# Gates spread by 16-bit products in three parts, an input stage that starts from the unnormalised x, and a last norm in two halves

## The chip, the cores and the metric

The kernel runs on one core of a Trainium2 chip. The metric is the device time of one execution in microseconds (us). The engines of the core that matter here are TensorE (PE, matrix products into PSUM), VectorE (DVE), ScalarE (ACT), GpSimd (POOL) and SyncE (SP), which issues most of the transfers.

## What is computed

Two layers over 512 tokens of width 1024, each a mixer (a recurrence and a state-space part), a cross-attention to 256 memory rows, and a large key-addressed feed-forward layer, called peer; a norm closes the whole. Cut to what the change touches:

```python
def rmsnorm(x, g):
    y = xf * lax.rsqrt(jnp.mean(xf * xf, axis=-1, keepdims=True) + RMS_EPS)
    return (y * g.astype(jnp.float32)).astype(x.dtype)

h = rmsnorm(x, norm_mix[l]);  z = h @ w_in[l]          # input stage of the mixer
...
top, pos = lax.top_k(cand, PEER_TOPK)                   # peer: 8 heads x 16 experts of 128 x 128
eidx = jnp.take_along_axis(cidx, pos, axis=-1)
gate = jax.nn.softmax(top, axis=-1)
act = jax.nn.gelu(jnp.einsum('thkd,td->thk', ue, hc).astype(jnp.float32))
return jnp.einsum('thk,thkd->td', (gate * act).astype(ve.dtype), ve)
...
return rmsnorm(x, norm_final)
```

## The kernel before, in words

Activations lie transposed: 128 partitions are a slice of the features, and 512 tokens lie along the free axis. The order of each engine's work is written out by hand, and semaphores tie the engines together. Large fp32 products are made of three 32-bit-rounded ones: each operand is split in a high and a low part (`split_high` on ScalarE, line 195; `split_low` on VectorE, line 200) and `product` (lines 207 to 209) issues high x high, low x high, high x low.

**Input stage** (`front`). ScalarE squares x, TensorE sums the squares over the partitions with a matrix of ones (L358), VectorE makes the mean, ScalarE its root, VectorE the reciprocal (L503) and h = x * gain * rstd (L505), and both split h. Only then can the first of 18 weight tiles be multiplied (24 matmuls of 512 columns each). Two PSUM banks take the tiles in turn; ScalarE copies each result out (`take`, L416, or L411, which writes with a wide step, for the last four), and VectorE shifts, mixes and prepares the recurrence.

**Peer**. The layer is computed densely for 384 of the 512 tokens: 128 tiles of `peer_u` give the activations (phase up, 24 matmuls of 384 columns each), and 128 tiles of `peer_v` are added up with weights (phase down). The weights are gate times activation, so the 16 x 8 gates of a token have to be spread over a 128 x 128 table. That is done in the middle of phase up, for 24 groups of 16 tokens: `route` holds, for each of a token's 128 picks (the partition) the first key, the second key and the gate. VectorE makes a one-hot of the first key (`one`), a one-hot of the second key times the gate (`two`), each 128 x 2048 in fp32 (`make_onehots`, L2417 to L2419), and TensorE multiplies the two for each token (`spread_gates`, L2162): 16 matmuls a group, which in fp32 run as 32 passes. ScalarE moves the sums to `gates_out` (L2260), and SyncE stores them to HBM. Around this VectorE works in a fixed order: one-hots of the next group, the low part of one or two weight tiles (`lows`), one gathered expert row for the remaining 128 tokens (`rows`, L2352, fetched by GpSimd). TensorE works on one or two up tiles, then a spread, and so on; three groups come with four tiles.

**End**. `norm` works on all 512 tokens at once, then one transfer of 2 MB stores the output.

## Time and profile before

| | us |
|---|---|
| median of 2 runs (4155.95 and 4173.33) | 4164.64 |
| the profiled execution, its own time | 4179.48 |
| its span, first to last instruction | 4177.7 |
| TensorE busy | 3788.4 (91%) |
| VectorE busy | 3029.4 (73%) |
| ScalarE busy | 1375.9 (33%) |

Busy is the time in which an engine has an instruction in work; matmul records overlap each other, so that a busy TensorE need not be one at its peak. The granted clock of TensorE was 0.949 of full speed in the mean. The columns of each view are told with its first rows below.

### The profile page before, as it was taken

The page shows a single profiled execution, that of the slowest core. Times are in us where ns is not written, and L with a number is a line of the kernel's source. Part 1 is how long each engine was busy: PE and PEld are TensorE (multiplying, and loading weights), DVE is VectorE, ACT ScalarE, POOL GpSimd, SP SyncE. Part 2 cuts the span into 40 slices and gives each one's busy share as a digit, 9 for nine tenths or more (in the row PEclk, how much of TensorE's full clock was granted, in tenths as well). Part 3 has the DMA queues.
Part 4 walks back from the last instruction along what each step waited for, and adds up shares of the span by engine and source line. Part 5 has one row for each costly group of instructions (what it writes and reads, how often), then busy time and mean ns, then how long its engine had stood idle before and what let it go on. Part 6 is the DMA issues. An engine that isn't in the chain of part 4 may idle for free. (4 is left out here: it accounts for less than half of the span.)

```text
span 4177.7 us, 67901 instructions
## 1 busy us (share of the span) xinstructions
PE 3788.4 (91%) x27802; PEld 3460.6 (83%) x27802; DVE 3029.4 (73%) x5310; ACT 1375.9 (33%) x2109; POOL 869.4 (21%) x593
## 2 busy tenths in 40 slices
PE   6878889899998998999999888989999999999997
PEld 4547777699998998999986776669999898899996
DVE  6446455489888987877775646458888897877876
ACT  3442123333333432333334213333333343333332
POOL 3000000011102234444430000001111223544542
PEclk8989989999999999999999989999999999999998
DMA  4741212167776789999961022227777679999994
GB/s 151 262 144 35 99 54 99 61 206 206 208 209 208 270 319 355 338 337 343 349 246 61 22 99 71 91 72 220 211 209 212 213 264 335 359 342 340 338 340 183
DMA packets 319480, 885.61 MB, mean 212 GB/s; under 512 B 29473, under 2 KB 156577, under 8 KB 311745
## 3 DMA queue, kind: packets, MB, share of 16 engines
q1 hardware_dynamic: 245440, 612.80, 43.9%
q0 software_dynamic: 73728, 268.47, 18.0%
q8 instruction: 219, 3.59, 0.4%
q14 instruction: 93, 0.75, 0.1%
HBM read 751.13 MB, written 130.02 MB: 211 GB/s over the span
## 5 line engine op out<-in xcount | busy, mean ns | idle before, releaser
L207 PE MATMUL peer_ps<-peer_h_high,tile_high 128*128 128x384 f32 (+1 forms) x2304 | 797.3, 346 | 35.5 <-DVE peer_h_low L200 16.6
L207 PE MATMUL peer_ps<-gate_high,tile_high 128*128 128x384 f32 x2048 | 709.6, 347 | 96.9 <-DVE tile_low L200 96.8
L2120 POOL DMA_INDIRECT row<-in_peer_u_rows,row_at x256 | 380.9, 1488 | 1969.0 <-DVE row L2352 1202.1
L209 PE MATMUL peer_ps<-peer_h_high,tile_low 128*128 128x384 f32 (+1 forms) x2304 | 788.5, 342 | 0.0
L208 PE MATMUL peer_ps<-peer_h_low,tile_high 128*128 128x384 f32 (+1 forms) x2304 | 788.3, 342 | 0.0
L200 DVE TENSOR_TENSOR tile_low<-tile,tile_high 128x1024 fp32r<-128x1024 f32 x544 | 662.4, 1220 | 157.0 <-ACT tile_high L195 152.2
L208 PE MATMUL peer_ps<-gate_low,tile_high 128*128 128x384 f32 x2048 | 704.0, 344 | 0.0
L209 PE MATMUL peer_ps<-gate_high,tile_low 128*128 128x384 f32 x2048 | 702.9, 343 | 0.0
L195 ACT ACTIVATE tile_high<-tile 128x1024 fp32r<-128x1024 f32 x544 | 571.2, 1050 | 20.1 <-DMA tile<-in_peer_u 19.9
L2120 POOL DMA_INDIRECT row<-in_peer_v,row_at x256 | 454.6, 1776 | 480.0 <-DVE own_sum L2358 437.3
L207 PEld LDWEIGHTS peer_ps<-gate_high,tile_high 128*128 128x128 f32 x2048 | 398.1, 194 | 107.6 <-DVE tile_low L200 107.5
L207 PEld LDWEIGHTS peer_ps<-peer_h_high,tile_high 128*128 128x128 f32 x2304 | 435.5, 189 | 58.3 <-issue 32.6
L209 PEld LDWEIGHTS peer_ps<-peer_h_high,tile_low 128*128 128x128 f32 x2304 | 435.1, 189 | 10.7
L208 PEld LDWEIGHTS peer_ps<-peer_h_low,tile_high 128*128 128x128 f32 x2304 | 435.6, 189 | 9.6
L195 ACT ACTIVATE gate_high<-weighed 128x384 fp32r<-128x384 f32 x256 | 134.6, 526 | 804.5 <-DMA tile<-in_peer_v 480.2
L208 PEld LDWEIGHTS peer_ps<-gate_low,tile_high 128*128 128x128 f32 x2048 | 398.1, 194 | 0.0
L209 PEld LDWEIGHTS peer_ps<-gate_high,tile_low 128*128 128x128 f32 x2048 | 397.3, 194 | 0.0
L2239 ACT ACTIVATE up_act<-peer_ps 128x384 f32<-128x384 f32 x240 | 118.6, 494 | 811.4 <-DMA acts<-up_act 561.6
L2358 DVE SCALAR_TENSOR_TENSOR own_sum<-row,row_dots,own_sum 128x1024 f32<-128x1024 f32 x254 | 324.8, 1279 | 5.6
L2352 DVE SCALAR_TENSOR_TENSOR row<-row,h_own 128x1024 f32<-128x1024 f32 x256 | 307.7, 1217 | 3.6 <-DMA row<-in_peer_u_rows,row_at 3.6
L200 DVE TENSOR_TENSOR gate_low<-weighed,gate_high 128x384 fp32r<-128x384 f32 x256 | 141.4, 552 | 229.6 <-ACT tile_high L195 228.9
L2162 PE MATMUL peer_ps<-onehot_gates,onehot 128*128 128x128 f32 x1536 | 183.4, 277 | 10.4 <-ACT gates_out L2260 10.4
(453 smaller groups left out, 5476.2 us busy)
## 6 DMA issues: line engine op xcount, KB each, us to landing
tile<-in_peer_u SPq DMA_DIRECT2D x256, 512.0 KB, 4.1
tile<-in_peer_v SPq DMA_DIRECT2D x256, 512.0 KB, 7.1
gates<-gates_out SPq DMA_DIRECT2D x24, 2048.0 KB, 10.1
gates_in<-gates SPq DMA_DIRECT2D x32, 1536.0 KB, 15.9
acts<-up_act SPq DMA_DIRECT2D x240, 192.0 KB, 4.4
act_in<-acts SPq DMA_DIRECT2D x240, 192.0 KB, 8.8
in_w<-in_w_in SPq DMA_DIRECT2D x36, 512.0 KB, 3.6
tile<-in_peer_wq SPq DMA_DIRECT2D x32, 512.0 KB, 4.8
```

The source lines that it names most:

```text
L195: return act.activation(out, value, ACT.Copy)
L200: return dve.tensor_tensor(out, value, high.bitcast(F32), ALU.subtract)
L207: pe.matmul(out, wh, mh, start=first, stop=False)
L208: pe.matmul(out, wh, ml, start=False, stop=False)
L209: return pe.matmul(out, wl, mh, start=False, stop=last)
L2120: pool.indirect_dma_start(row[n % NROW][:, :], None, table, bass.IndirectOffsetOnAxis(ap=row_at[:, n % ROWS:n % ROWS + 1], axis=0)) \
L2162: last = pe.matmul(ps[2 + n % GBANKS][:, t * NKEY:(t + 1) * NKEY], one[g % 2][:, 4 * c + t, :], two[g % 2][:, 4 * c + t, :], start=True, s ...
L2239: act.activation(up[i % 2][:, :], ps[m % NPS][:, 0:TD], ACT.Gelu_apprx_tanh).then_inc(taken.sem, 1)
L2352: last = dve.scalar_tensor_tensor(out=x, in0=x, scalar=1.0, in1=h_own[:, :], op0=ALU.mult, op1=ALU.mult, accum_out=dots[:, j:j + 1])
L2358: last = dve.scalar_tensor_tensor(out=own_sum[:, :], in0=x, scalar=dots[:, j:j + 1], in1=own_sum[:, :], op0=ALU.mult, op1=ALU.add)
```

## The change

Three edits that do not depend on each other.

**Gates.** `route`, the one-hots and the ramp of keys become bf16, and the token index becomes the innermost one of the one-hots ([128 keys, 16 tokens] instead of [16 tokens, 128 keys]). So that nothing of a gate is lost it is split in three bf16 parts (`share_gates`), VectorE multiplies the second one-hot by each part (three products in place of one), and TensorE adds three bf16 matmuls per token in PSUM, in place of one fp32 matmul of two passes. It reads both operands with a step of 16 elements, 32 bytes.

**Input.** The tiles are multiplied by x * gain; rstd, which depends on the token alone, is multiplied in when a result is taken out of PSUM, now by VectorE. The first tile goes ahead of the sum of squares on TensorE.

**Last norm.** Mean, root, reciprocal and scaling go by halves of 256 tokens, and the output is stored in eight pieces as they are made.

```diff
-def norm(pg, src, gain, dst, n, early=None):
+def final_norm(pg, out):
...
+        @block.sync
+        def _(sp):
+            for h in range(2):
+                for k in range(KD):
+                    sp.wait_ge(scaled.sem, scaled.at(h * KD + k + 1))
+                    if k % 2:
+                        sp.dma_start(out[:, k - 1:k + 1, halves[h]], y[:, k - 1:k + 1, halves[h]]).then_inc(stored.sem, 16)
+            sp.wait_ge(stored.sem, stored.at(16 * KD))
...
-            act.wait_ge(meaned.sem, meaned.at(1))
-            act.activation(root[:, :], rstd[:, :], ACT.Sqrt).then_inc(rooted.sem, 1)
+                act.activation(sq[:, k, :], pg.xT[:, k, :], ACT.Square).then_inc(squared.sem, 1)
+            for h in range(2):
+                act.wait_ge(meaned.sem, meaned.at(h + 1))
+                act.activation(root[:, halves[h]], rstd[:, halves[h]], ACT.Sqrt).then_inc(rooted.sem, 1)
...
-            for k in range(KD):
-                pe.wait_ge(squared.sem, squared.at(k + 1))
-                last = pe.matmul(ps[:, :], pg.c["ones"][:, :], sq[:, k, :], start=(k == 0), stop=(k == KD - 1))
-            last.then_inc(summed.sem, 1)
+            for h in range(2):
+                for k in range(KD):
+                    pe.wait_ge(squared.sem, squared.at(k + 1))
+                    last = pe.matmul(ps[h][:, :], pg.c["ones"][:, :], sq[:, k, halves[h]], start=(k == 0), stop=(k == KD - 1))
+                last.then_inc(summed.sem, 1)
...
+
+            def mean(h):
+                dve.wait_ge(summed.sem, summed.at(h + 1))
+                dve.tensor_scalar(rstd[:, halves[h]], ps[h][:, :], 1.0 / D, RMS_EPS, ALU.mult, ALU.add).then_inc(meaned.sem, 1)
+
+            mean(0)
+            for h in range(2):
+                dve.wait_ge(rooted.sem, rooted.at(h + 1))
+                link(dve.reciprocal(rstd[:, halves[h]], root[:, halves[h]]))
+                if h == 0:
+                    mean(1)
+                for k in range(KD):
+                    dve.scalar_tensor_tensor(out=y[:, k, halves[h]], in0=pg.xT[:, k, halves[h]], scalar=gain[:, k:k + 1],
+                                             in1=rstd[:, halves[h]], op0=ALU.mult, op1=ALU.mult).then_inc(scaled.sem, 1)
...
+            tile(0)
             for k in range(KD):
                 pe.wait_ge(squared.sem, squared.at(k + 1))
                 last = pe.matmul(ps[7][:, :], pg.c["ones"][:, :], sq[:, k, :], start=(k == 0), stop=(k == KD - 1))
...
             for j in range(IN_TILES):
-                tile(j)
+                if j:
+                    tile(j)
...
-            def take(j):
-                act.wait_ge(in_summed.sem, in_summed.at(j + 1))
...
+            def scaled_high(k):
+                act.activation(rh[:, k, :], pg.xT[:, k, :], ACT.Copy, scale=gain[:, k:k + 1]).then_inc(h_high_made.sem, 1)
...
+            for k in range(4):
+                scaled_high(k)
+            high(0)
+            for k in range(4, KD):
+                scaled_high(k)
             for k in range(KD):
                 act.activation(sq[:, k, :], pg.xT[:, k, :], ACT.Square).then_inc(squared.sem, 1)
-            for j in range(2):
-                high(j)
+            high(1)
+            high(2)
             act.wait_ge(meaned.sem, meaned.at(1))
             act.activation(root, rstd, ACT.Sqrt).then_inc(rooted.sem, 1)
-            high(2)
-            for k in range(KD):
-                act.wait_ge(h_scaled.sem, h_scaled.at(k + 1))
-                split_high(act, rh[:, k, :], h[:, k, :]).then_inc(h_high_made.sem, 1)
             for j in range(IN_TILES):
-                take(j)
                 if j + IN_SPLIT < IN_TILES:
                     high(j + IN_SPLIT)
...
-                split_low(dve, rl[:, k, :], h[:, k, :], rh[:, k, :]).then_inc(h_low_made.sem, 1)
+                dve.scalar_tensor_tensor(out=rl[:, k, :], in0=pg.xT[:, k, :], scalar=gain[:, k:k + 1], in1=rh[:, k, :].bitcast(F32),
+                                         op0=ALU.mult, op1=ALU.subtract).then_inc(h_low_made.sem, 1)
...
+            def take(j):
+                i = IN_ORDER[j]
+                dve.wait_ge(in_summed.sem, in_summed.at(j + 1))
+                if i >= RW_TILES:
+                    tokens = lambda x: x.rearrange("p (n s) -> p n s", s=SC)
+                    dve.tensor_tensor(uT[:, i - RW_TILES, :].rearrange("p (s n) -> p n s", s=SC), tokens(ps[j % 2][:, :]), tokens(rstd),
+                                      ALU.mult).then_inc(in_taken.sem, 1)
+                    return
+                if j >= IN_ZB:
+                    dve.wait_ge(shifted.sem, shifted.at(j - IN_ZB + 1))
+                dve.tensor_tensor(zb[j % IN_ZB][:, 1:T + 1], ps[j % 2][:, :], rstd, ALU.mult).then_inc(in_taken.sem, 1)
...
+            for k in range(4):
+                h_left(k)
             weight_low(0)
+            for k in range(4, KD):
+                h_left(k)
+            weight_low(1)
             dve.wait_ge(summed.sem, summed.at(1))
             dve.tensor_scalar(rstd, ps[7][:, :], 1.0 / D, RMS_EPS, ALU.mult, ALU.add).then_inc(meaned.sem, 1)
-            weight_low(1)
+            weight_low(2)
...
             dve.wait_ge(rooted.sem, rooted.at(1))
             link(dve.reciprocal(rstd, root))
-            for k in range(KD):
-                dve.scalar_tensor_tensor(out=h[:, k, :], in0=pg.xT[:, k, :], scalar=gain[:, k:k + 1], in1=rstd,
-                                         op0=ALU.mult, op1=ALU.mult).then_inc(h_scaled.sem, 1)
-                if k >= 2:
-                    h_left(k - 2)
-            h_left(KD - 2)
...
             for j in range(IN_TILES):
+                take(j)
                 if j < RW_TILES:
                     shift(j)
...
+PLANES = 3
...
-        route = buf("route", [P, 3, TD])
+        route = buf("route", [P, 2 + PLANES, TD], BF16)
+        gate_row = buf("gate_row", [P, TD])
...
-            one = [buf(f"onehot{b}", [P, GROUP, NKEY], own=own) for b in range(2)]
-            two = [buf(f"onehot_gates{b}", [P, GROUP, NKEY], own=own) for b in range(2)]
+            one = [buf(f"onehot{b}", [P, NKEY, GROUP], BF16, own=own) for b in range(2)]
+            two = buf("onehot_second", [P, NKEY, GROUP], BF16, own=own)
+            shares = [buf(f"onehot_gates{b}", [P, PLANES, NKEY, GROUP], BF16, own=own) for b in range(2)]
+            key_ramp = buf("key_ramp", [P, NKEY, GROUP], BF16, own=own)
+            left = buf("gates_left", [P, TD], own=own)
...
-                        last = pe.matmul(ps[2 + n % GBANKS][:, t * NKEY:(t + 1) * NKEY], one[g % 2][:, 4 * c + t, :],
-                                         two[g % 2][:, 4 * c + t, :], start=True, stop=True)
+                        for j in range(PLANES):
+                            last = pe.matmul(ps[2 + n % GBANKS][:, t * NKEY:(t + 1) * NKEY], one[g % 2][:, :, 4 * c + t],
+                                             shares[g % 2][:, j, :, 4 * c + t], start=(j == 0), stop=(j == PLANES - 1))
                     last.then_inc(spread.sem, 1)
...
-                        act.activation(route[:, :, tb * P:(tb + 1) * P], bank[:, 0:3, :], ACT.Copy).then_inc(flip_taken.sem, 1)
+                        act.activation(route[:, 0:3, tb * P:(tb + 1) * P], bank[:, 0:3, :], ACT.Copy)
+                        act.activation(gate_row[:, tb * P:(tb + 1) * P], bank[:, 2, :], ACT.Copy).then_inc(flip_taken.sem, 1)
...
+            def share_gates():
+
+                link(dve.tensor_tensor(left[:, :], gate_row[:, :], route[:, 2, :], ALU.subtract))
+                link(dve.tensor_copy(route[:, 3, :], left[:, :]))
+                link(dve.tensor_tensor(left[:, :], left[:, :], route[:, 3, :], ALU.subtract))
+                link(dve.tensor_copy(route[:, 4, :], left[:, :]))
...
             def make_onehots(g):
                 t = slice(g * GROUP, (g + 1) * GROUP)
                 if g >= 2:
                     dve.wait_ge(spread.sem, spread.at((g - 1) * (GROUP // 4)))
-                per_key = lambda j: route[:, j, t].rearrange("p (t k) -> p t k", k=1).to_broadcast([P, GROUP, NKEY])
-                keys_at = pg.c["ramp"][:, :].rearrange("p (t k) -> p t k", t=1).to_broadcast([P, GROUP, NKEY])
-                dve.tensor_tensor(two[g % 2][:, :, :], keys_at, per_key(1), ALU.is_equal)
-                link(dve.tensor_tensor(one[g % 2][:, :, :], keys_at, per_key(0), ALU.is_equal))
-                last = dve.tensor_tensor(two[g % 2][:, :, :], two[g % 2][:, :, :], per_key(2), ALU.mult)
+                per_key = lambda j: route[:, j, t].rearrange("p (k t) -> p k t", k=1).to_broadcast([P, NKEY, GROUP])
+                if g:
+                    dve.wait_ge(onehots_made.sem, onehots_made.at(g))
+                dve.tensor_tensor(two[:, :, :], key_ramp[:, :, :], per_key(1), ALU.is_equal)
+                link(dve.tensor_tensor(one[g % 2][:, :, :], key_ramp[:, :, :], per_key(0), ALU.is_equal))
+                for j in range(PLANES):
+                    last = dve.tensor_tensor(shares[g % 2][:, j, :, :], two[:, :, :], per_key(2 + j), ALU.mult)
                 last.then_inc(onehots_made.sem, 1)
...
+            share_gates()
+            link(dve.tensor_copy(key_ramp[:, :, :], pg.c["ramp"][:, :].rearrange("p (k t) -> p k t", t=1)
+                                 .to_broadcast([P, NKEY, GROUP])))
             make_onehots(0)
```

How the instructions move. On VectorE in peer, one group of 16 tokens and what follows it (the numbers behind the names are those of buffers; `row` is a gathered expert row, `tile` a weight tile). Before:

```order
L2417 TENSOR_TENSOR onehot_gates_209<-ramp,route 128x2048 [waits spread]
L2418 TENSOR_TENSOR onehot_207<-ramp,route 128x2048
L2419 TENSOR_TENSOR onehot_gates_209<-onehot_gates_209,route 128x2048 [waits vec_step]
L200 TENSOR_TENSOR tile_low_168<-tile_162,tile_high_165 128x1024 [waits tile_high_made]
L2352 SCALAR_TENSOR_TENSOR row_184,row_dots<-row_184,h_own 128x1024 [waits row_loaded5]
L2417 TENSOR_TENSOR onehot_gates_210<-ramp,route 128x2048 [waits spread]
```

and in the changed kernel:

```order
L2453 TENSOR_TENSOR onehot_second<-key_ramp,route 128x2048 [waits onehots_made,spread]
L2454 TENSOR_TENSOR onehot_209<-key_ramp,route 128x2048
L2456 TENSOR_TENSOR onehot_gates_212<-onehot_second,route 128x2048 [waits vec_step]
L2456 TENSOR_TENSOR onehot_gates_212<-onehot_second,route 128x2048 x2
L210 TENSOR_TENSOR tile_low_169<-tile_163,tile_high_166 128x1024 [waits tile_high_made]
L2380 SCALAR_TENSOR_TENSOR row_186,row_dots<-row_186,h_own 128x1024 [waits row_loaded5]
L2453 TENSOR_TENSOR onehot_second<-key_ramp,route 128x2048 [waits onehots_made,spread]
```

Three instructions of a group have become five, the first of them waits also for the group before.

On TensorE, one spread with the last matmul of the tile ahead of it. Before:

```order
L209 MATMUL peer_ps_229<-peer_h_high,tile_low_168 128x384
L2162 MATMUL peer_ps_230<-onehot_gates_209,onehot_207 128x128 [waits onehots_made]
L2162 MATMUL peer_ps_230<-onehot_gates_209,onehot_207 128x128 x3
L2162 MATMUL peer_ps_231<-onehot_gates_209,onehot_207 128x128 x4
L2162 MATMUL peer_ps_232<-onehot_gates_209,onehot_207 128x128 x4
L2162 MATMUL peer_ps_233<-onehot_gates_209,onehot_207 128x128 x4
```

and in the changed kernel, where 16 matmuls (in fp32 of two passes each) are 48:

```order
L219 MATMUL peer_ps_234<-peer_h_high,tile_low_169 128x384
L2189 MATMUL peer_ps_235<-onehot_gates_212,onehot_209 128x128 [waits onehots_made]
L2189 MATMUL peer_ps_235<-onehot_gates_212,onehot_209 128x128 x11
L2189 MATMUL peer_ps_236<-onehot_gates_212,onehot_209 128x128 x12
L2189 MATMUL peer_ps_237<-onehot_gates_212,onehot_209 128x128 x12
L2189 MATMUL peer_ps_238<-onehot_gates_212,onehot_209 128x128 x12
```

On VectorE at the start of the input stage, before:

```order
L200 TENSOR_TENSOR in_w_low_57<-in_w_51,in_w_high_54 128x1024 [waits tile_high_made]
L500 TENSOR_SCALAR v<-front_ps_71 128x512 [waits norm_summed]
L200 TENSOR_TENSOR in_w_low_58<-in_w_52,in_w_high_55 128x1024 [waits tile_high_made]
L503 RECIPROCAL v<-v 128x512 [waits norm_rooted]
L505 SCALAR_TENSOR_TENSOR mixT<-xT,vec,v 128x512 [waits vec_step]
L505 SCALAR_TENSOR_TENSOR mixT<-xT,vec,v 128x512 x2
L200 TENSOR_TENSOR in_rl<-mixT,in_rh 128x512 [waits act_high_made]
L505 SCALAR_TENSOR_TENSOR mixT<-xT,vec,v 128x512
L200 TENSOR_TENSOR in_rl<-mixT,in_rh 128x512 [waits act_high_made]
```

and in the changed kernel:

```order
L492 SCALAR_TENSOR_TENSOR in_rl<-xT,vec,in_rh 128x512 [waits act_high_made] x4
L210 TENSOR_TENSOR in_w_low_57<-in_w_51,in_w_high_54 128x1024 [waits tile_high_made]
L492 SCALAR_TENSOR_TENSOR in_rl<-xT,vec,in_rh 128x512 [waits act_high_made] x4
L210 TENSOR_TENSOR in_w_low_58<-in_w_52,in_w_high_55 128x1024 [waits tile_high_made]
L521 TENSOR_SCALAR in_rstd<-front_ps_72 128x512 [waits norm_summed]
L210 TENSOR_TENSOR in_w_low_59<-in_w_53,in_w_high_56 128x1024 [waits tile_high_made]
L528 RECIPROCAL in_rstd<-v 128x512 [waits norm_rooted]
L505 TENSOR_TENSOR zb_60<-front_ps_65,in_rstd 128x512 [waits tile_summed,cleared,vec_step]
L510 TENSOR_TENSOR wag<-zb_60 128x512 [waits tile_taken]
L511 SCALAR_TENSOR_TENSOR wag<-wag,vec,zb_60 128x512 [waits vec_step]
L210 TENSOR_TENSOR in_w_low_57<-in_w_51,in_w_high_54 128x1024 [waits tile_high_made]
```

The splits no longer wait for the norm; the mean and the reciprocal come behind them, and each result is taken by VectorE (L505) ahead of its shift.

## Rows read from the trace of the kernel before

**Rows 1.** The profile page, engines: busy us, share, instructions

```profile
PE 3788.4 (91%) x27802; PEld 3460.6 (83%) x27802; DVE 3029.4 (73%) x5310; ACT 1375.9 (33%) x2109; POOL 869.4 (21%) x593
```

**Rows 2.** Stretches while gates are spread: busy us, clock, DMA share, GB/s

```profile
core 0: us, PE busy (x) PEld busy (x) DVE busy (x) ACT busy (x) POOL busy (x), PEclk, DMA share, GB/s
1400.00:1420.00 20.00, 20.00 (x140) 20.00 (x139) 19.93 (x14) 10.05 (x18) 7.47 (x3) 1.00 0.78 272
```

**Rows 3.** Timeline, VectorE, spreading: start us, us, instruction, [idle before]

```profile
1407.96 2.28 DVE L2417 TENSOR_TENSOR onehot_gates<-ramp,route 128x2048 f32<-128x2048 f32 x1
1410.16 2.28 DVE L2418 TENSOR_TENSOR onehot<-ramp,route 128x2048 f32<-128x2048 f32 x1
1412.48 2.29 DVE L2419 TENSOR_TENSOR onehot_gates<-onehot_gates,route 128x2048 f32<-128x2048 f32 x1
1414.69 1.22 DVE L200 TENSOR_TENSOR tile_low<-tile,tile_high 128x1024 fp32r<-128x1024 f32 x1
1415.83 1.22 DVE L2352 SCALAR_TENSOR_TENSOR row<-row,h_own 128x1024 f32<-128x1024 f32 x1
...
1436.13 2.29 DVE L2417 TENSOR_TENSOR onehot_gates<-ramp,route 128x2048 f32<-128x2048 f32 x1
```

**Rows 4.** Timeline, TensorE: a 384-column product, then two spreads

```profile
1341.60 0.33 PE L207 MATMUL peer_ps<-peer_h_high,tile_high 128*128 128x384 f32 x1
...
1342.12 0.33 PE L207 MATMUL peer_ps<-peer_h_high,tile_high 128*128 128x384 f32 x1
...
1508.06 3.73 PE L2162 MATMUL peer_ps<-onehot_gates,onehot 128*128 128x128 f32 x32
...
1515.80 3.73 PE L2162 MATMUL peer_ps<-onehot_gates,onehot 128*128 128x128 f32 x32
```

**Rows 5.** Groups of instructions, VectorE, 2048 elements: busy us, mean ns

```profile
L2418 DVE TENSOR_TENSOR onehot<-ramp,route 128x2048 f32<-128x2048 f32 x48 | 109.6, 2283 | 0.0
...
L1638 DVE COPY s_keep<-s_small 128x2048 f32<-128x2048 f32 x1 | 1.2, 1226 | 0.0
```

**Rows 6.** Groups, ScalarE and VectorE, 512 elements, with and without a wide step

```profile
L416 ACT ACTIVATE zb<-front_ps 128x512 f32<-128x512 f32 x28 | 16.7, 598 | 104.9 <-PE front_ps L209 104.9
...
L411 ACT ACTIVATE mixT<-front_ps 128x512 f32<-128x512 f32 x8 | 8.8, 1094 | 52.3 <-PE front_ps L209 52.3
...
L1180 DVE TENSOR_TENSOR rk<-mixT,s_turns 128x512 f32<-128x512 f32 x8 | 8.8, 1097 | 12.2 <-ACT s_turns L1087 12.2
```

**Rows 7.** Timeline, start of the input stage, layer 0

```profile
229.83 4.27 ACT L432 ACTIVATE rk<-xT 128x512 f32<-128x512 f32 x8 [17.03 <-PEq L1248]
...
257.26 0.60 ACT L416 ACTIVATE zb<-front_ps 128x512 f32<-128x512 f32 x1 [2.37 <-PE front_ps L209]
```

**Rows 8.** Timeline, start of cross-attention, layer 0

```profile
659.62 2.56 ACT L1820 ACTIVATE xa_h_high<-xT,vec 128x512 fp32r<-128x512 f32 x4 [11.89 <-PEq L892]
...
673.33 7.03 PE L1788 MATMUL xa_ps<-xa_q,ones 128*128 128x512 f32 x16
...
679.79 0.79 PE L207 MATMUL xa_ps<-xa_h_high,xa_w_high 128*128 128x512 f32 x1
...
682.13 3.35 DVE L1913 RECIPROCAL xa_rstd<-xa_root 128x512 f32<-128x512 f32 x1
```

**Rows 9.** Timeline, last norm and store; the group of 256-element reciprocals

```profile
4149.92 4.27 ACT L166 ACTIVATE norm_sq<-xT 128x512 f32<-128x512 f32 x8 [18.18 <-PEq L2010]
...
4164.77 5.39 DVE L185 SCALAR_TENSOR_TENSOR yT<-xT,vec,norm_rstd 128x512 f32<-128x512 f32 x8
...
4171.03 0.34 SPq L2560 DMA_DIRECT2D out<-yT  x1
...
L1546 DVE RECIPROCAL mem_rstd<-mem_root 128x256 f32<-128x256 f32 x1 | 1.8, 1753 | 0.1
```

**Rows 10.** Timeline, VectorE, end of the input stage, layer 1

```profile
2338.77 2.28 DVE L564 TENSOR_TENSOR rk<-rk,cum 128x2048 f32<-128x2048 f32 x1
...
2353.01 2.48 DVE L580 TENSOR_TENSOR e<-front_ps,v 128x512 f32<-128x512 f32 x4
```

More of the change, by code:

```diff
@@ L361, in _ @@
             for j in range(IN_TILES):
-                tile(j)
+                if j:
+                    tile(j)
                 if j in LORA_AFTER:
                     if j == 5 and layer:
+                        pe.wait_ge(v1_scaled.sem, v1_scaled.at(1))
                         for k in range(KD):
-                            last = pe.matmul(ps[7][0:32, :], v1[:, k, :], h[:, k, :], start=(k == 0), stop=(k == KD - 1))
+                            last = pe.matmul(ps[7][0:32, :], v1[:, k, :], pg.xT[:, k, :], start=(k == 0), stop=(k == KD - 1))
                         last.then_inc(v1_summed.sem, 1)
@@ L526, in _ @@
                     link(last)
+                if j == 6 and layer:
+                    dve.wait_ge(v1_summed.sem, v1_summed.at(1))
+                    dve.tensor_tensor(vl[:, :], ps[7][0:32, :], rstd[0:32], ALU.mult).then_inc(v1_taken.sem, 1)
                 if j == 6:
@@ L581, in _ @@
                     link(last)
[L582 removed]
+    for s, n in ((squared, KD), (summed, 1), (meaned, 1), (rooted, 1), (v1_scaled, 1 if layer else 0), (h_high_made, KD), (h_low_made, KD),
                  (high_made, IN_TILES), (low_made, IN_TILES), (in_summed, IN_TILES), (in_taken, IN_TILES), (shifted, RW_TILES),
@@ L2552, in build @@
             peer(pg, layer)
[L2553 to L2561 removed]
+        final_norm(pg, out)
 def kernel(**inputs):
```

61 lines of the change are left out of this document (14 added, 47 removed).

## The prediction, made before the changed kernel ran

> **What bounds the kernel now.** I read the engines' shares first. TensorE is busy for 91% of the span and VectorE for 73% [rows 1], but these are means over stages, so I went to the three places that the change touches. While gates are spread, both are full: in a typical 20 us TensorE has 20.00 and VectorE 19.93 us of work in hand, at full clock, with DMA at 0.78 [rows 2]. Which of them sets the pace is read from their timelines. VectorE starts one-hots at 1407.96 and, three groups later, at 1436.13 [rows 3]: 28.17 us for three groups with four weight tiles, with no idle time noted. On TensorE two high x high products, three matmuls apart, start 0.52 us apart, so a 384-column matmul takes 0.173 us and a tile of 24 takes 4.15. From spread to spread with one tile between them it is 7.74 us [rows 4]; that leaves 3.59 for the 32 passes of a spread, 0.112 each. Three groups cost TensorE 4 x 4.15 + 3 x 3.59 = 27.4 us. So VectorE bounds this stage by 0.8 us in 28: the reader should see that a saving on VectorE alone is worth almost nothing, and that the price of a spread on TensorE decides. The stage is 24 groups in each of two layers, 16 times three groups, 450 us.
>
> At the start of the input stage TensorE waits for the norm: 27.4 us from the first square to the first tile taken [rows 7]. The end is a chain of one engine after the other [rows 9].
>
> **Gates, VectorE.** A group has three operations of 2.28 us that start 2.20 or, behind a wait for the one before, 2.32 apart; with the last, 6.73 us [rows 3]. They become five, of 16-bit elements. No row shows VectorE on such operands. The upper bound is the fp32 operation, 2.28 us for 2048 elements; the lower one is the fp32 copy, 1.23 us, two elements a step [rows 5]. I take the lower: the copy moves 8 bytes per element, in and out, and a product with three 16-bit operands moves 6. Then the five start 1.14 or 1.26 apart, 5.8 us, and a group gives back 0.9: three groups are 25.4 us. The Trainium skill (VectorE: DVE Perf Modes, The perf-mode tier table) has 1224 ns for a bf16 `tensor_tensor` of this size; no run here shows it yet.
>
> **Gates, TensorE.** 32 passes become 48 (the order shows 12 matmuls per bank for 4). What does a bf16 pass of 128 columns cost? The lower bound is by columns: 0.173 us for 384 is 0.058 for 128 if all scales; with some 0.01 that does not scale, 0.065. The nearest row by shape is the fp32 pass itself, 0.112. The upper bound comes from the wide step: ScalarE takes 1094 ns to write 512 elements with a step of 256 bytes and 598 without one, and VectorE 1097 ns to read 512 of them, nearly what 1024 plain ones take [rows 3, 6]. That is 1.0 ns more per element, or 1.8 to 2.1 in all; 128 columns are 0.19 us a pass if 1.0 ns is added to 0.065, and 0.24 at 1.85 ns in all. Both operands of the new matmuls have a step of 32 bytes. I take 0.065, since TensorE reads a 4-byte column in 0.42 ns where a bf16 column has 2 bytes, and both ends stay for the range. Three groups are then 4 x 4.15 + 144 x 0.065 = 26.0 us, above VectorE's 25.4, so TensorE would set the pace: 28.17 - 26.0 = 2.2 us, 16 times, **-35**. Not all of it comes: the split of the gates (four short operations), the ramp's copy (1.2 to 2.3 us) and ScalarE's three extra copies stand ahead of the first one-hots; less what the first group is quicker, that is about 3.5 us a layer, **+7**. Gates: -28. What follows, phase down, is unchanged and starts earlier by as much. ScalarE's work, 10 us in 20, and the stores cover nothing that becomes late.
>
> The Trainium skill (TensorE: Matmul & The Clock Gate, Back-to-back issue gap) gives about 81 ns for a matmul of 128 columns with its weight load. By that three groups are 16.6 + 11.7 = 28.3 us, and the gates would bring nothing. No pair of this kind is in the trace.
>
> **Input stage.** Cross-attention in this trace already works in the new order: scaled high parts first, tile 0, then the sum of squares. There tile 1 starts 20.2 us after ScalarE's first instruction (659.62 to 679.79), and the reciprocal ends at 25.9, before tile 1 is through [rows 8]. In the input stage tile 1 starts at 27.4 [rows 7]. I take the difference, 7.2 us a layer, **-14**. Against it: 18 takes move from ScalarE to VectorE, 0.7 us each and about 1.1 for the four with a wide step [rows 6]. Mostly TensorE's tiles (24 x 0.227 = 5.4 us) cover them. Where VectorE is the late one, in the middle of the stage, some 0.8 us a layer is added. At the end of layer 1 it works from 2338.77 to 2355.5 without a stop [rows 10], and the take of tile 15 now stands behind 9 us of it, while tile 17 waits for that bank: about 3 us. **+4.5** in all. The extra product on v1 is short and hidden by the wait for the root.
>
> **Last norm.** Now 20.2 us from the first square to the last scaled tile, then 0.9 to the issue and 6.7 to the end of the span [rows 9]. With halves: squares 4.3, root of half 0 by 6, reciprocal 1.75 [rows 9], scaling 3.2, a mean 0.4, then 1.75 + 3.2 for half 1: 16.3 us, and a last piece of 256 KB in place of 2 MB, perhaps 3.5 with its issue. 27.8 becomes 19.8, **-8**.
>
> **Sum** against the profiled execution: 4179.5 - 28 - 9.5 - 8 = 4134. That execution is 14.8 us above the median of the runs shown; on the median's footing it is 4164.6 - 45.5 = **4119**.
>
> **Rivals.**
> - *The gates bring nothing* (a pass at about 0.080): -10 to -18 us in all, about 4150. Against it, the column rate of rows 4; for it, that a weight load is no cheaper than it was.
> - *A bf16 pass costs as much as an fp32 one*, 0.112: 16.6 + 16.2 = 32.8 us for three groups, +74 us, with the rest 4221. For it: the weights of 128 columns are loaded in each pass, and the wide step may take back what 2-byte columns give.
> - *Slower*: the wide step costs TensorE per element what it costs the others. 0.19 to 0.24 a pass make 44 to 51 us of three groups, +250 to +370, so 4400 to 4515. It sets in, for the whole kernel, above 0.124 a pass, where the gates alone cost 100 us. For it, two engines agree on the price [rows 6]; against it, one of these is a write, both are fp32, and TensorE is another reader. The Trainium skill (SBUF — State Buffer, Specifications) says that full bandwidth needs at least two hits in each line of 16 bytes; a step of 32 bytes has one. Whether TensorE feels that, no row here shows.
> - *VectorE gains nothing from 16 bits*: 2 x 2.2 us more per group, 48 times, +211, with the rest 4360.
>
> **Chances.** The forecast's case 0.46, no gain from the gates 0.10, pass as before 0.24, wide step 0.13, VectorE at the old rate 0.07. The first three, 0.80, lie between 4085 (VectorE-bound, 44 us from the gates, the others a little better) and 4250, which is my range; the forecast's case by itself has 4085 to 4140. Two per cent, about what a measurement of this kernel can tell from no change, is 83 us: faster than 4081 has 0.08, a corner of the first case; slower than 4248 has 0.22, the last two cases and an edge of the third; within it 0.70.
>
> **What would show it.** The spread in the changed trace: 48 passes in about 3.1 us; 5.4 would be the second rival, 9 or more the third. VectorE's 2048-element operations at 1.22 us, or at 2.28. The distance of one-hot starts over three groups, 26.0. Tile 1 of the input stage 20 us after its start. At the end, 20 us from the first square. I am wrong if a pass is above 0.08, if TensorE's clock drops in the stage because it now waits, or if takes on VectorE hold tiles up elsewhere in the input stage.

## The result: 8.9% slower, and the profile after

The changed kernel takes 4534.98 us in the median of two runs (4531.09 to 4538.86), the kernel before 4164.64: a ratio of 1.089, with a 95% interval of 1.078 to 1.100. I had forecast 4119 with a range of 4085 to 4250. The profiled execution after is the one of 4538.86 us, against 4179.5 before: +359.4. It is the rival of the wide step that happened, a little dearer than I had priced it.

The page of the changed kernel: engines, the granted clock and DMA share in 40 slices, then the groups of the spread and of VectorE's first 16-bit operation of a group (busy us, mean ns, idle before and its releaser).

```profile
PE 4187.9 (92%) x28586; PEld 3661.5 (81%) x28586; DVE 3013.9 (66%) x5448; ACT 1376.2 (30%) x2079; POOL 791.8 (17%) x593
...
PEclk8899999999977779999999989999997777999999
...
L2189 PE MATMUL peer_ps<-onehot_gates,onehot 128*128 128x128 bf16 x2304 | 562.8, 423 | 3.9 <-DVE onehot_gates L2456 3.9
...
L2453 DVE TENSOR_TENSOR onehot_second<-key_ramp,route 128x2048 bf16<-128x2048 bf16 x48 | 58.8, 1225 | 414.8 <-PE peer_ps L2189 414.6
```

TensorE gained 400 us of busy time where [rows 1] has 3788.4, and VectorE fell from 73% to 66%. VectorE's operation takes 1225 ns where the fp32 one took 2283 [rows 5], as forecast. But ahead of the one-hots of a group it now waits for TensorE, 414.6 us in all. In the kernel before, the same wait came to 3.4:

```profile
L2417 DVE TENSOR_TENSOR onehot_gates<-ramp,route 128x2048 f32<-128x2048 f32 x48 | 109.7, 2286 | 3.5 <-PE peer_ps L2162 3.4
```

The clock has two troughs of four slices, and these are the two stages in which gates are spread.

TensorE's timeline in one of them (start us, us, instruction); a spread, five of the 24 products behind it and the next spread:

```profile
1411.64 11.71 PE L2189 MATMUL peer_ps<-onehot_gates,onehot 128*128 128x128 bf16 x48
1422.98 0.69 PE L217 MATMUL peer_ps<-peer_h_high,tile_high 128*128 128x384 f32 x1
1423.47 0.52 PE L218 MATMUL peer_ps<-peer_h_low,tile_high 128*128 128x384 f32 x1
1423.79 0.52 PE L219 MATMUL peer_ps<-peer_h_high,tile_low 128*128 128x384 f32 x1
...
1425.70 0.34 PE L219 MATMUL peer_ps<-peer_h_high,tile_low 128*128 128x384 f32 x1
1425.87 0.33 PE L217 MATMUL peer_ps<-peer_h_high,tile_high 128*128 128x384 f32 x1
...
1428.50 11.73 PE L2189 MATMUL peer_ps<-onehot_gates,onehot 128*128 128x128 bf16 x48
```

From the start of a spread to the next product is 11.34 us for 48 passes, **0.236 us each**; the spreads in [rows 4] were 3.73 us long. The products behind it start 0.32 us apart at first and 0.173 later. The clock explains that second, smaller loss. Stretches through the same spread (busy us of each engine, granted clock, DMA share, GB/s):

```profile
1413.00:1415.00 2.00, 2.00 (x10) 1.21 (x9) 1.85 (x3) 0.51 (x2) 0.00 (x0) 1.00 0.23 27
1415.00:1417.00 2.00, 2.00 (x10) 1.24 (x9) 0.00 (x0) 0.37 (x1) 0.94 (x1) 0.61 0.74 274
1417.00:1419.00 2.00, 2.00 (x10) 1.28 (x9) 0.00 (x0) 0.60 (x1) 0.00 (x0) 0.50 0.94 293
...
1423.00:1425.00 2.00, 2.00 (x8) 2.00 (x7) 1.61 (x2) 0.60 (x1) 0.00 (x0) 0.50 0.00 0
```

The clock is full (2.4 GHz) at the start of the spread and falls to half (1.2 GHz) some 4 us into it. Ten passes lie in or across each stretch of 2 us at either level (8.5 of them start in it, at 0.236 us each), so the pass doesn't wait for the array; it waits for something that the clock doesn't touch. What the low level costs comes afterwards: the tile behind a spread takes 5.5 us (1422.98 to 1428.50) in place of 4.15.

VectorE over one group (start us, us, instruction, [idle before and releaser]) has its work for a group done and waits for a buffer of the spread; the first line is the start of the group ahead, the last one that of the third group after it:

```profile
1406.68 1.23 DVE L2453 TENSOR_TENSOR onehot_second<-key_ramp,route 128x2048 bf16<-128x2048 bf16 x1 [11.86 <-PE peer_ps L2189]
...
1423.39 1.22 DVE L2453 TENSOR_TENSOR onehot_second<-key_ramp,route 128x2048 bf16<-128x2048 bf16 x1 [8.54 <-PE peer_ps L2189]
1424.53 1.22 DVE L2454 TENSOR_TENSOR onehot<-key_ramp,route 128x2048 bf16<-128x2048 bf16 x1
1425.78 3.50 DVE L2456 TENSOR_TENSOR onehot_gates<-onehot_second,route 128x2048 bf16<-128x2048 bf16 x3
...
1461.39 1.22 DVE L2453 TENSOR_TENSOR onehot_second<-key_ramp,route 128x2048 bf16<-128x2048 bf16 x1 [11.82 <-PE peer_ps L2189]
```

One-hots start at 1406.68 and, three groups later, at 1461.39: 54.7 us where [rows 3] gives 28.17.

**The balance**, read as the first and last start of the matmuls of each stage in both profiled executions. First to last spread: before 1304.8 to 1527.0 and 3269.8 to 3494.8 (222.2 and 225.0 us), after 1283.0 to 1712.9 and 3434.4 to 3863.3 (429.9 and 428.9): +411.6. Input stage, first ScalarE instruction to last product: -7.1 and -2.6. Last gate product to the end: -5.9. The scan stage, between the last product of the input and the first of the tail, which the change doesn't touch: 205.1 and 207.7 before, 193.0 and 193.1 after, -26.7. The small rest, -9.9, is spread over the other stages. 411.6 - 9.7 - 5.9 - 26.7 - 9.9 = +359.4. Two things were to be explained: the price of the pass, and 27 us that nobody had asked for.

### The profile page after: what moved, and what is told of

The parts are those of the page before. It is cut to its first block and busy times, and to the rows that moved or that the text cites. A ratio compares the mean times of both kernels' runs of the same rounds, so it can differ in the third digit from the quotient of the medians.

```text
span 4537.1 us, 69625 instructions
## 1 busy us (share of the span) xinstructions
PE 4187.9 (92%) x28586; PEld 3661.5 (81%) x28586; DVE 3013.9 (66%) x5448; ACT 1376.2 (30%) x2079; POOL 791.8 (17%) x593
## 5 line engine op out<-in xcount | busy, mean ns | idle before, releaser
L217 PE MATMUL peer_ps<-peer_h_high,tile_high 128*128 128x384 f32 (+1 forms) x2304 | 826.4, 359 | 24.8 <-DVE peer_h_low L210 16.4
L218 PE MATMUL peer_ps<-peer_h_low,tile_high 128*128 128x384 f32 (+1 forms) x2304 | 812.0, 352 | 0.0
L219 PE MATMUL peer_ps<-peer_h_high,tile_low 128*128 128x384 f32 (+1 forms) x2304 | 808.5, 351 | 0.0
L2146 POOL DMA_INDIRECT row<-in_peer_u_rows,row_at x256 | 310.4, 1213 | 2420.3 <-DVE row L2380 1668.3
L2189 PE MATMUL peer_ps<-onehot_gates,onehot 128*128 128x128 bf16 x2304 | 562.8, 423 | 3.9 <-DVE onehot_gates L2456 3.9
L2189 PEld LDWEIGHTS peer_ps<-onehot_gates,onehot 128*128 128x128 bf16 x2304 | 338.4, 149 | 212.3 <-issue 7.2
L217 PEld LDWEIGHTS peer_ps<-peer_h_high,tile_high 128*128 128x128 f32 x2304 | 456.7, 198 | 49.0 <-issue 25.7
L218 PEld LDWEIGHTS peer_ps<-peer_h_low,tile_high 128*128 128x128 f32 x2304 | 454.7, 197 | 9.6
L219 PEld LDWEIGHTS peer_ps<-peer_h_high,tile_low 128*128 128x128 f32 x2304 | 453.8, 197 | 10.7
L2453 DVE TENSOR_TENSOR onehot_second<-key_ramp,route 128x2048 bf16<-128x2048 bf16 x48 | 58.8, 1225 | 414.8 <-PE peer_ps L2189 414.6
```

Source lines behind the costliest of these rows:

```text
L217: pe.matmul(out, wh, mh, start=first, stop=False)
L218: pe.matmul(out, wh, ml, start=False, stop=False)
L219: return pe.matmul(out, wl, mh, start=False, stop=last)
L2146: pool.indirect_dma_start(row[n % NROW][:, :], None, table, bass.IndirectOffsetOnAxis(ap=row_at[:, n % ROWS:n % ROWS + 1], axis=0)) \
L2189: last = pe.matmul(ps[2 + n % GBANKS][:, t * NKEY:(t + 1) * NKEY], one[g % 2][:, :, 4 * c + t], shares[g % 2][:, j, :, 4 * c + t], start=( ...
L2453: dve.tensor_tensor(two[:, :, :], key_ramp[:, :, :], per_key(1), ALU.is_equal)
```

## Experiments

Theory: the pass costs 0.236 us because the elements of its operands lie 32 bytes apart. Rivals: 48 short 16-bit passes cost that by their number, weight loads or accumulation; or the low clock is the cause and not a consequence; or part of the loss sits in the input stage or the last norm.

### e1: gates as before, the other two parts as changed

```diff
-            one = [buf(f"onehot{b}", [P, NKEY, GROUP], BF16, own=own) for b in range(2)]
+            one = [buf(f"onehot{b}", [P, GROUP, NKEY], own=own) for b in range(2)]
...
-                        for j in range(PLANES):
-                            last = pe.matmul(..., one[g % 2][:, :, 4 * c + t], shares[g % 2][:, j, :, 4 * c + t], ...)
+                        last = pe.matmul(..., one[g % 2][:, 4 * c + t, :], two[g % 2][:, 4 * c + t, :], ...)
```

> The changed kernel with the gates of the kernel before (one-hots in fp32, one product a token, each token's 128 elements side by side), its input stage and its last norm as changed. Theory (the whole loss lies in the gates): the two stages 222 and 225 us from first to last spread as before, the rest as after, so 4539 - 412 = about 4127 us profiled, 0.985 to 0.993 of the kernel before. If the scan stage of the changed kernel was shorter only by the clock it happened to get (27 us over both layers), that may be missing: 4154. Rival (the input stage or the last norm costs part of it): above 4180.

Measured: 4137.55 us, ratio 0.9948 (0.9924 to 0.9973); profiled 4127.4. Spreads over 222.2 and 221.8 us. The whole loss is in the gates, and the other two parts together are a small gain, some 20 us. The profiled time is the one expected; the ratio lies just above the 0.985 to 0.993 that I had expected.

### e2 to e4: which operand's step is paid for

```diff
+flat = lambda x, n: x.rearrange("p k t -> p (k t)")[:, n * NKEY:(n + 1) * NKEY]
...
-                            last = pe.matmul(..., one[g % 2][:, :, 4 * c + t],
-                                             shares[g % 2][:, j, :, 4 * c + t], ...)
+                            last = pe.matmul(..., flat(one[g % 2][:, :, :], 4 * c + t),
+                                             flat(shares[g % 2][:, j, :, :], 4 * c + t), ...)
```

e2 has both edits, e3 only that of `one` (the weights), e4 only that of `shares` (the moving operand, the one that streams through the array). VectorE still writes the old layout, so the gates come out as other numbers and only the times of these three count.

> The changed kernel, all instructions the same, but TensorE reads both operands of the 48 passes of a group from 128 elements that lie side by side, so the gates are other numbers. Theory (the step of 32 bytes between elements is what a pass costs): pass 0.06 to 0.09 us, spread of a group 3 to 4 us in place of 11.4, three groups 26 to 28 us in place of 53.8, VectorE's wait for spreads gone, the clock of the tile behind a spread full; time 4539 - 16 x 27 = about 4105 to 4140 us. Rival (48 short passes in 16 bits cost this whatever the step, by their number, their weight loads or PSUM accumulation): 0.237 us a pass, 4535 us. Rival (the low clock is the cause): pass as at full clock from the start of a spread, which was 0.2 us too, so no change.

> As e2, but only the one-hots of the first keys, which are loaded as weights, are read side by side; the moving operand keeps its step of 32 bytes. If each operand pays for its own step and the reads follow one another (0.237 = 2 x 0.118): 0.17 to 0.18 us a pass, 8.4 us a spread. If the moving operand alone pays: 0.237. If the weights alone pay: under 0.09.

> As e2, but only the moving operand is read side by side; the weights keep the step of 32 bytes. If each operand pays for its own step and the reads follow one another: 0.17 to 0.18 us a pass. If the moving operand alone pays: under 0.09. If the weights alone pay: 0.237.

Measured: e2 4105.02 us, ratio 0.9878 (0.9848 to 0.9908). One run each: e3 4525.07, e4 4108.19. The groups of the spread in layer 0, of e2, e3 and e4 in turn:

```profile
L2190 PE MATMUL peer_ps<-onehot_gates,onehot 128*128 128x128 bf16 x1152 | 69.0, 219 | 7.3 <-ACT gates_out L2288 5.4 <-DVE onehot_gates L2457 2.0
```

```profile
L2190 PE MATMUL peer_ps<-onehot_gates,onehot 128*128 128x128 bf16 x1152 | 271.1, 411 | 2.0 <-DVE onehot_gates L2457 2.0
```

```profile
L2190 PE MATMUL peer_ps<-onehot_gates,onehot 128*128 128x128 bf16 x1152 | 77.0, 227 | 2.0 <-DVE onehot_gates L2457 2.0
```

The same 1152 passes are 69, 271 and 77 us of TensorE. The number of passes, their weight loads and the accumulation are the same in all three, so none of them is the cause. And the two steps aren't paid for alike: the **moving operand's alone** makes the pass. The weights' step adds 8 us in 1152 passes. By the time from the start of a spread to the next product, a pass is 0.228 us in e3 and 0.063 in e4:

```profile
1406.80 11.30 PE L2190 MATMUL peer_ps<-onehot_gates,onehot 128*128 128x128 bf16 x48
1417.73 0.69 PE L217 MATMUL peer_ps<-peer_h_high,tile_high 128*128 128x384 f32 x1
```

```profile
1396.57 3.20 PE L2190 MATMUL peer_ps<-onehot_gates,onehot 128*128 128x128 bf16 x48
1399.58 0.42 PE L217 MATMUL peer_ps<-peer_h_high,tile_high 128*128 128x384 f32 x1
```

I had no row that told the two apart, and that each would pay half was one of the possibilities. In e2 the clock in the stage is 0.99, in the changed kernel 0.71. As the pass took the same at both levels there, the low clock follows from the slow pass and doesn't cause it.

### e5 to e8: how the price goes with the step

The one-hots, shares and ramp are laid out as blocks of SUB tokens; e5 has SUB = 4, e6 1, e7 2, e8 8, and the changed kernel is 16. The step between two elements of a token is SUB times 2 bytes, and VectorE meets runs of SUB elements.

```diff
-            one = [buf(f"onehot{b}", [P, NKEY, GROUP], BF16, own=own) for b in range(2)]
+            one = [buf(f"onehot{b}", [P, GROUP // SUB, NKEY, SUB], BF16, own=own) for b in range(2)]
...
-                                             shares[g % 2][:, j, :, 4 * c + t], ...)
+                                             shares[g % 2][:, j, (4 * c + t) // SUB, :, (4 * c + t) % SUB], ...)
```

> The changed kernel with one-hots, shares and ramp laid out as blocks of 4 tokens (block, key, token in the block), so that both operands of a pass have a step of 4 elements, 8 bytes, and VectorE writes and reads runs of 4 elements. The whole computation is done. Theory A (TensorE's moving operand is read in pieces of 16 bytes, of which a step of 8 leaves two elements each, one of 32 one element): 0.12 us a pass, 5.8 us a spread, three groups 16.6 + 17.4 = 34 us, +6 on the 28 of before, 4107 + 16 x 8 = about 4235 us. Theory B (no step up to 16 bytes costs more than side by side): 0.06 to 0.07 us a pass, about 4105 us. Theory C (any step other than one element costs the full price): 0.235, 4535 us. VectorE: 1.22 us an operation if runs of 4 keep its rate, else 2.28, and then 3 x 2.2 + 15 x 2.28 = 41 us for three groups, near 4320 us.

> The same with blocks of 1 token: each token's 128 elements side by side, as before the change, in 16 bits. TensorE: 0.06 us a pass. VectorE reads the routing values with a step of zero in the innermost direction. If that keeps the rate of two elements a cycle: 1.22 us an operation and the time of e2, 4105 us. If it halves it: 2.28 us, a group's five operations 11.3 us, three groups 34 + 7 = 41 us, VectorE-bound, 16 x 13 more than before: about 4330 us.

> The same with blocks of 2 tokens, step of 4 bytes. Theory A: four elements in 16 bytes, 0.06 to 0.07 us a pass. Theory B: the same. Theory C: 0.235. VectorE with runs of 2 elements: 1.22 us if the pair of 16-bit elements in 4 bytes is what its rate wants, else 2.28.

> The same with blocks of 8 tokens, step of 16 bytes. Theory A: one element in each 16 bytes, 0.235 us a pass as with 32. Theory B: 0.06 to 0.07. Theory C: 0.235. If the price goes by distance on and on: half of that of 32 bytes, 0.12. VectorE 1.22 us an operation.

Measured, with the pass as the time from the start of a 48-pass spread to the next product, over 48. Both operands have the step; that the moving one pays is taken over from e3 and e4, which tried it at 32 bytes only.

| step | kernel | us a pass | VectorE op, us | clock in the stage | time, us | ratio (95%) |
|---|---|---|---|---|---|---|
| 2 bytes | e6 | 0.055 | 2.287 | 0.83 | 4358.4 | 1.048 (1.045 to 1.051) |
| 4 bytes | e7 | 0.057 | 1.221 | 0.98 | 4096.3, one run | |
| 8 bytes | e5 | 0.117 | 1.221 | 1.00 | 4197.0 | 1.010 (1.006 to 1.014) |
| 16 bytes | e8 | 0.231 | 1.221 | 0.72 | 4539.8, one run | |
| 32 bytes | changed kernel | 0.236 | 1.225 | 0.71 | 4535.0 | 1.089 (1.078 to 1.100) |

TensorE's rows of e7, e5 and e8, in this order (start us, us, instruction; the product behind the spread):

```profile
1426.41 2.94 PE L2190 MATMUL peer_ps<-onehot_gates,onehot 128*128 128x128 bf16 x48
1429.15 0.42 PE L217 MATMUL peer_ps<-peer_h_high,tile_high 128*128 128x384 f32 x1
```

```profile
1422.43 5.87 PE L2190 MATMUL peer_ps<-onehot_gates,onehot 128*128 128x128 bf16 x48
1428.05 0.42 PE L217 MATMUL peer_ps<-peer_h_high,tile_high 128*128 128x384 f32 x1
```

```profile
1425.05 11.46 PE L2190 MATMUL peer_ps<-onehot_gates,onehot 128*128 128x128 bf16 x48
1436.14 0.68 PE L217 MATMUL peer_ps<-peer_h_high,tile_high 128*128 128x384 f32 x1
```

Theory A holds at each step for the pass. 128 elements 16 bytes apart are 128 pieces of 16 bytes, 1.80 ns each; 8 bytes apart they are 64 pieces at 1.83 ns; 4 bytes apart, 32 pieces, which at that rate is 0.058 us and no more than the pass takes anyway. Beyond 16 bytes distance costs almost nothing more (0.231, 0.236). The theory of no price up to 16 bytes and that of one price for any step both fall. With 2-byte elements alone, a piece of 16 bytes and one of 8 elements are the same thing; these runs don't tell them apart. The times of the kernel were forecast less well than the passes: e5 came 38 us under the 4235 expected, e6 28 us over its 4330. The Trainium skill (SBUF — State Buffer, Specifications) asks for two hits in each line of 16 bytes for full bandwidth. The trace agrees on the 16 bytes, not on the two: a step of 8 bytes has two elements in a line and takes twice as long as one of 2 or 4.

e6 shows why the layout was turned at all. With each token's keys side by side VectorE reads the routing values with an innermost step of zero, and its operation takes 2.287 us, no faster than fp32; TensorE idles there, 219.5 us busy in 310, and its clock is 0.83. The group of e6 in layer 0 (busy us, mean ns, idle before):

```profile
L2457 DVE TENSOR_TENSOR onehot_gates<-onehot_second,route 128x2048 bf16<-128x2048 bf16 x72 | 160.7, 2287 | 0.8
```

So the two engines want opposite things, and two elements side by side, 4 bytes, content both: VectorE 1.221, TensorE 0.057.

### e9: the step of 4 bytes, timed

The kernel of e7.

> The kernel of e7 again (blocks of 2 tokens, a step of 4 bytes, all else as changed, the whole computation done), now timed against the kernel before. The one look gave 4096.3 us; the time in its gates, 203.6 and 203.3 us from first to last spread, is the time of e2 with both operands side by side. Theory: it keeps the forecast gain of the gates beside those of the input and the last norm, 4085 to 4110 us, ratio 0.982 to 0.988. Rival (the look was a lucky one): no better than e1, ratio 0.992 to 0.997.

Measured: 4099.19 us, ratio 0.9865 (0.9842 to 0.9889). It beats both kernels: 1.35% under the one before and, between two groups of runs, 9.6% under the changed one. 1.35% is a small gain, but the interval leaves 1 far out. Spreads take 204.7 and 202.5 us against 222.2 in e1: the forecast gain of the gates is there, 37 us over both layers between first and last spread; the rest of the 1.35% is the gain that e1 has too.

### e10 and e11: the input stage alone, and the kernel before once more

e10 is the kernel before with the diff's part in the input stage only. Its core:

```diff
-                act.activation(zb[j % IN_ZB][:, 1:T + 1], ps[j % 2][:, :], ACT.Copy).then_inc(in_taken.sem, 1)
...
+                dve.tensor_tensor(zb[j % IN_ZB][:, 1:T + 1], ps[j % 2][:, :], rstd, ALU.mult).then_inc(in_taken.sem, 1)
```

> The kernel before with only its input stage changed; gates and last norm as before. Theory (the input stage brings 10 us over both layers, the last norm 6): ratio to before 0.997 to 0.998, some 4 to 8 us over e1. If the scan stage behind it owes its 13 us a layer to the input stage, that gain is here too, and the ratio is 0.991 to 0.996, with scan stages of 190 to 194 us. Rival: the scan stage's shorter time belongs to single executions, and these show 205 us in some of them whatever the input stage.

> The kernel before, unchanged, for a second trace of it. If the scan stage (last product of the input to the first product of the tail) costs 205 us in the kernel before as such, it shows 205 to 208 us in both layers again. If the first trace was one in which the clock had fallen by chance, it shows about 193 us, and the span is near 4150.

Measured: e10 4150.22 us, ratio 0.9980 (0.9963 to 0.9998). e11, one run, 4167.14. The scan stage in e10 takes 204.7 us in layer 0 and 189.9 in layer 1; in e11 205.0 and 206.7. That alone would let one believe that the input stage shortens it. The same kernel twice says otherwise. First and last start of the last input products and the first tail products of layer 1, of e7 and of e9, which are one program:

```profile
L217 PE MATMUL front_ps<-in_rh,in_w_high x144: 387/389/795, 2149.8 to 2312.0; 128*128 128x512 f32 x144
L217 PE MATMUL tail_ps<-kk_rounded,rk_rounded x16: 389/391/500, 2502.4 to 2514.9; 128*128 128x512 f32 x16
```

```profile
L217 PE MATMUL front_ps<-in_rh,in_w_high x144: 387/389/797, 2159.8 to 2320.8; 128*128 128x512 f32 x144
L217 PE MATMUL tail_ps<-kk_rounded,rk_rounded x16: 389/389/500, 2527.6 to 2540.4; 128*128 128x512 f32 x16
```

190.4 us in the one, 206.8 in the other. The two executions were on different chips, but e10 has both lengths within one execution. Where the time goes is seen in layer 0 of the same two, where the stage takes 192.9 and 203.6. The lines are one of four groups of 128 small matmuls that follow each other there; the last three of the four are long in e9:

```profile
L999 PE MATMUL tail_ps<-mixT,cum x128: 270/270/318, 512.6 to 516.9; 32*128 32x64 f32 x128
```

```profile
L999 PE MATMUL tail_ps<-mixT,cum x128: 416/416/468, 515.7 to 523.6; 32*128 32x64 f32 x128
```

The group takes 4.3 us (512.6 to 516.9) or 7.9 (515.7 to 523.6), at full clock or at half, by the execution. The rival of e10 holds: 11 to 16 us a layer belong to single executions. In all the traces the stage is 203 to 208 us long where this group ran at half clock and 188 to 198 where it ran at full. With the input stage of before, that was half clock in both layers of the two traces of the kernel before, and full clock in both layers of e12 (192.7 and 198.1 us); so the old input stage doesn't force the low level. With the changed input stage it was half clock in 5 of 22 layers. Whether the change makes it rarer is open: six layers are too few. It would be part of what e1 has beyond its stages.

### e12: a wide step with fp32

```diff
-            one = [buf(f"onehot{b}", [P, GROUP, NKEY], own=own) for b in range(2)]
-            two = [buf(f"onehot_gates{b}", [P, GROUP, NKEY], own=own) for b in range(2)]
+            one = [buf(f"onehot{b}", [P, NKEY, GROUP], own=own) for b in range(2)]
+            two = [buf(f"onehot_gates{b}", [P, NKEY, GROUP], own=own) for b in range(2)]
```

> The kernel before with its fp32 one-hots laid out key by key (step of 16 elements, 64 bytes) in place of token by token; the whole computation is done. If TensorE reads its moving operand in pieces of 16 bytes at 1.84 ns each, as e5, e7 and e8 show (0.122, 0.062, 0.238 us a pass of 128 elements), and reads an fp32 operand once: 0.235 us a pass, 7.5 us a spread of 32 passes; the three groups 16.6 + 3 x 7.5 + about 3 of low clock = 42 us, +14 x 16, about 4380 us. If it reads it twice or more for fp32: 0.47 us a pass or more, 4740 us or more. If the piece is not 16 bytes but 8 elements: the same 0.235. VectorE's operations 2.28 us as before.

Measured, one run: 4272.37 us. The spread, TensorE's timeline:

```profile
1400.29 7.12 PE L2162 MATMUL peer_ps<-onehot_gates,onehot 128*128 128x128 f32 x32
1407.09 0.51 PE L207 MATMUL peer_ps<-peer_h_high,tile_high 128*128 128x384 f32 x1
```

6.80 us for 32 passes, 0.213 each; in the kernel before, the same measure (1515.80 to 1519.29) gives 0.109, and the prediction had 0.112 from [rows 4]. With one element in each piece, an fp32 pass costs about what a 16-bit one does, a little less even. So the width of an element is not what is paid for, and the theory that an fp32 operand is read twice, at 0.47, falls. Whether a piece ends after 16 bytes or after 8 elements this run can't tell, as the expectation said. My time was 108 us too high. Of this, 48 are the debt of low clock that I had added, 3 us in three groups: the clock stays at 1.00 in this stage (stretch 1400 to 1440). Another 34 are the pass itself, 0.7 us a spread. The scan stage, which met the full clock, was 21 us shorter than in e11. Why 0.213 and not 0.231 stays open.

## Why the prediction was wrong, point by point

- **What bounds the stage** was read rightly: VectorE by little, TensorE close behind, so that the price of a pass decides. It did.
- **Gates, VectorE**: 1.14 to 1.26 us apart, 5.8 a group, as forecast (1.22 us an operation). The Trainium skill (VectorE: DVE Perf Modes, The perf-mode tier table) gives 1224 ns; the trace has 1225.
- **Gates, TensorE, the step that failed**: "I take 0.065, since TensorE reads a 4-byte column in 0.42 ns where a bf16 column has 2 bytes". It measured 0.236, the upper bound that stood beside it. The sentence argues from bytes, and bytes were not the matter: side by side a pass takes 0.055 (e2, e6), and this estimate was good for that case alone. The column rate came from rows whose operands lie side by side, and the changed operands don't. The only rows on a wide step [rows 6] said 1.8 to 2.1 ns an element, 0.24 a pass at 1.85; TensorE's is 1.84. That the three engines share one cause no run shows, so the close agreement may be luck. I set them aside as being other engines, and gave 0.13 to the case that all the evidence on the step spoke for. -35 became +412.
- **The slower rival** had the right mechanism and the right price of a pass, 0.19 to 0.24, but 44 to 51 us for three groups where 54.7 came. What was missing is the clock: each spread leaves the tile behind it 1.2 to 1.4 us longer, about 4 in three groups. "TensorE's clock drops in the stage because it now waits" stood among the things that would make me wrong, with no price. Hence 4535 beyond that rival's 4515.
- **The Trainium skill** (TensorE: Matmul & The Clock Gate, Back-to-back issue gap) has 81 ns for a matmul of 128 columns with its weight load. Here a pass is 0.055 to 0.057 us with a step of at most 4 bytes, so that figure, by which the gates would bring nothing, is too dear for this stream.
- **Set-up of the gates**, +7: not separated. In e9 the gates' total gain is 4137.6 - 4099.2 = 38 us, between different groups of runs, about what the two stages show between first and last spread, so no more than a few us.
- **Input stage**: tile 1 starts 19.6 us after ScalarE's first instruction, forecast 20 (in layer 0):

```profile
228.58 2.56 ACT L421 ACTIVATE in_rh<-xT,vec 128x512 fp32r<-128x512 f32 x4 [14.59 <-PEq L1269]
...
241.71 7.03 PE L369 MATMUL front_ps<-rk,ones 128*128 128x512 f32 x16
...
248.18 0.79 PE L217 MATMUL front_ps<-in_rh,in_w_high 128*128 128x512 f32 x1
```

  It answers to [rows 7]. In all -9.7 against -9.5 forecast, split as thought: -7.1 in layer 0 and -2.6 in layer 1, where the takes on VectorE cost more of it. e10 has 0.998 for the kernel, 8 us.
- **Last norm**: -5.9 against -8. The rows that answer to [rows 9]:

```profile
4515.25 4.27 ACT L171 ACTIVATE final_sq<-xT 128x512 f32<-128x512 f32 x8 [18.18 <-PEq L2032]
4515.93 9.93 PE L181 MATMUL final_ps<-final_sq,ones 128*128 128x256 f32 x32 [6.17 <-ACT final_sq L171]
...
4522.45 0.42 DVE L190 TENSOR_SCALAR final_rstd<-final_ps 128x256 f32<-128x256 f32 x1 [7.71 <-PE final_ps L181]
...
4525.98 0.42 DVE L190 TENSOR_SCALAR final_rstd<-final_ps 128x256 f32<-128x256 f32 x1 [0.87 <-PE final_ps L181]
4526.32 3.24 DVE L199 SCALAR_TENSOR_TENSOR final_y<-xT,vec,final_rstd 128x256 f32<-128x256 f32 x8
...
4531.26 3.25 DVE L199 SCALAR_TENSOR_TENSOR final_y<-xT,vec,final_rstd 128x256 f32<-128x256 f32 x8
```

  From the first square to the last scaled tile it is 19.3 us (4515.25 to 4531.26 + 3.25) where I had 16.3. I had counted from the squares' own 4.3 us; the sums take TensorE until 4522.4 for half 0 and 4525.9 for half 1, and the mean of half 1 stands ahead of the scaling of half 0 on VectorE and waits for them.
- **The footing**: 27 us of the difference of the two profiles come from the scan stage and are no effect of the gates. I had the profile 14.8 us above the median and could not say where. The low clock in the scan stage, 11 to 16 us a layer, is large enough for it; that it was the reason is not shown.

## What to carry to other kernels

When a layout is turned so that one engine finds its elements side by side, look at who else reads the buffer: give the rows on a step their weight in the price of the other reader, even if they are another engine's, before the rows on its plain rate. If both want the innermost place, give each a run: two 16-bit elements side by side kept VectorE's double rate and cost TensorE nothing, and turned a loss of 8.9% into a gain of 1.35%. And if only one operand must be spread out, let it be the weights: e4, with the step on the weights alone, took 4108 us in one run. Its gates are other numbers, so it shows the price and not a kernel to use.

## What the runs showed of the hardware

- TensorE's moving operand in 16 bits behaves as if read in pieces of 16 bytes at 1.80 to 1.84 ns a piece (1.78 with the weights side by side, e3). A pass of 128 columns is 0.055 us at a step of 2 bytes, 0.057 at 4, 0.117 at 8, 0.231 at 16 and 0.236 at 32. The slow passes take the same at full clock and at half; the 2-byte pass doesn't, it takes 0.106 at half (e6, 1288.43 to 1292.35). In fp32, a step of 64 bytes makes 0.213 of 0.109 (e12).
- A step of 32 bytes on the weights is nearly free: 0.063 us a pass in e4 where e2 has 0.055.
- TensorE was busy without a gap, yet with passes of 0.236 us its clock fell: full when a spread began, half some 4 us later, and full again some 3 us into the products behind it. With 0.231 a pass (e8) the stage has 0.72, with 0.228 (e3) 0.72 as well. At 0.117 a pass (e5, stretch 1290 to 1540) and in fp32 at 0.213 (e12) it has 1.00. The spreads of e12 are also shorter, 6.8 us against 11.1, and no run tells which of the two kept its clock up. Busy time in a profile doesn't show the difference; TensorE was busier after (92%) than before (91%).
- The same program meets full or half clock in the small matmuls of its scan stage, 11 to 16 us a layer, with no change of the code (e7 and e9).
